# A first and a second attention: dense units dealt over the slots of the last and ahead of the first pair of heads

## What is computed

```python
# first block
h = rmsnorm(x, g_norm);  proj = h @ w_in            # u, v, gate, q, k, v, b_gate, gate_logits
y_a = chunked_spatial_gating(gelu(u), gelu(v), ...) * silu(a_gate)
y_b = dilated_attention(q, k, v) * silu(b_gate)     # 16 heads of 64, softmax, three dilations
g_a, g_b = split(sigmoid(gate_logits), 2)
x = x + (g_a * (y_a @ w_proj_a) + g_b * (y_b @ w_proj_b)) @ w_out
# second block: a state-space mixer, then a per-layer embedding with a sigmoid gate
# third block: stick-breaking attention over shared keys and values
k = rmsnorm(kv[..., :1024] per head);  q = rmsnorm(q per head) / 8
z = q @ k.T;  keep = sigmoid(-z);  weights = sigmoid(z) * (product of keep over the later keys)
y = (weights @ v) * silu(gate);  x = x + y @ w_out
```

## Time and profile before

| | |
|---|---|
| three timed runs | 3404.18, 3405.32, 3412.97 us; median 3405.32 |
| the profiled execution | 3399.16 us; span from first to last instruction 3397.7 us |
| busy | PE 92%, DVE 54%, ACT 41%, POOL 20% of the span |
| mean granted TensorE clock | 0.96 of full speed |
| first attention, pairs 0 to 6 | about 560 to 1080 us of the span, 74.0 to 74.6 us each |
| its last pair and what follows to the next stage | 1080.4 to 1152.2 |
| the stage after it | 1152.2 to 1325.9 |
| second attention: dense units of pair 0 | 2438.5 to 2488.1 |
| its pairs 0 to 6, then pair 7 | 2511.9 to 3100.5, then to about 3178 |

### The profile page before, as it was taken

How to read it: one execution, slowest core, us unless ns; L and a number is a source line. 1 busy time by engine, 2 the same in 40 slices (tenths; PEclk the granted TensorE clock), 3 DMA queues, 4 the chain that set the end, 5 groups by cost and what they waited for, 6 DMA issues and landing times. The chain is left out here.

```text
span 3397.7 us, 42014 instructions
## 1 busy us (share of the span) xinstructions
PE 3130.8 (92%) x15516; PEld 2609.2 (77%) x15516; DVE 1840.8 (54%) x2484; ACT 1404.4 (41%) x2100; POOL 667.5 (20%) x448
## 2 busy tenths in 40 slices
PE   6999999999999799879999999998889999997799
PEld 5788887888887587657777878777678888886677
DVE  4344223666666423356757566675447766776343
ACT  3333213555555422234334252434246666666331
POOL 3100002222222000211001020100224444443110
PEclk8999999999999899879999999999889999998899
DMA  2111222111111223002111121211211111111221
GB/s 96 41 48 41 74 68 72 59 57 57 57 59 67 75 70 109 32 27 71 53 58 56 50 75 44 75 44 62 82 32 38 38 38 38 38 38 44 113 73 56
DMA packets 54602, 197.36 MB, mean 58 GB/s; under 512 B 6304, under 2 KB 9248, under 8 KB 54176
## 3 DMA queue, kind: packets, MB, share of 16 engines
q1 hardware_dynamic: 45600, 164.66, 14.4%
q0 software_dynamic: 8832, 30.41, 2.9%
HBM read 165.56 MB, written 21.10 MB: 55 GB/s over the span
## 5 line engine op out<-in xcount | busy, mean ns | idle before, releaser
L114 ACT ACTIVATE whi<-wraw 128x1024 fp32r<-128x1024 f32 x208 | 218.4, 1050 | 451.3 <-PE a_D L127 59.2
L119 DVE TENSOR_TENSOR wlo<-wraw,whi 128x1024 fp32r<-128x1024 f32 x176 | 247.9, 1409 | 176.0 <-ACT whi L114 172.7
L125 PE MATMUL b_D<-x1hi,whi 128*128 128x512 f32 x640 | 255.9, 400 | 8.5 <-DVEq L999 6.6
L125 PE MATMUL ssm_D<-x1hi,whi 128*128 128x512 f32 x640 | 259.0, 405 | 4.6 <-DVEq L1748 4.6
L127 PE MATMUL ssm_D<-x1hi,wlo 128*128 128x512 f32 x640 | 252.0, 394 | 0.0
L126 PE MATMUL ssm_D<-x1lo,whi 128*128 128x512 f32 x640 | 251.9, 394 | 0.0
L126 PE MATMUL b_D<-x1lo,whi 128*128 128x512 f32 x640 | 251.3, 393 | 0.0
L127 PE MATMUL b_D<-x1hi,wlo 128*128 128x512 f32 x640 | 250.8, 392 | 0.0
L2178 DVE TENSOR_TENSOR_SCAN stick_keep<-stick_keep 128x896 f32<-128x896 f32 (+7 forms) x128 | 209.0, 1637 | 37.1 <-ACT stick_keep L2093 35.9
L125 PE MATMUL stick_D<-x1hi,whi 128*128 128x512 f32 x512 | 210.7, 412 | 7.0 <-DVE x1lo L152 7.0
L2321 POOL TENSOR_TENSOR stick_rows<-stick_rows,stick_keep 128x896 f32<-128x896 f32 (+7 forms) x128 | 157.9, 1236 | 295.2 <-DVE stick_keep L2178 290.1
(11 more groups left out here) (400 smaller groups left out, 8010.0 us busy)
## 6 DMA issues: line engine op xcount, KB each, us to landing
wraw<-w_dram SPq DMA_DIRECT2D x208, 512.0 KB, 3.5
sq<-acum_rows SPq DMA_DIRECT2D x32, 512.0 KB, 3.8
att_bias<-alibi_dram SPq DMA_DIRECT2D x16, 512.0 KB, 3.5
stack<-stack POOLq DMA_DIRECT2D x32, 256.0 KB, 3.6
x_sb<-xT_dram SPq DMA_DIRECT2D x8, 512.0 KB, 7.9
branch_a<-sq POOLq DMA_DIRECT2D x8, 512.0 KB, 3.5
y_b<-att_y POOLq DMA_DIRECT2D x8, 512.0 KB, 3.0
f<-y_b SPq DMA_DIRECT2D x2, 2048.0 KB, 9.4
```

The costliest lines, as they stand in the source:

```text
L114: act.activation(self.whi[:, s, :, :], self.wraw[:, s, :, :], ACT.Copy).then_inc(self.w_hi, 1)
L119: dve.tensor_tensor(self.wlo[:, s, :, :], self.wraw[:, s, :, :], self.whi[:, s, :, :].bitcast(F32), ALU.subtract).then_inc(self.w_lo, 1)
L125: pe.matmul(out, self.whi[:, s, w0, :], xhi[:, k, cols], start=start, stop=False)
```

## The change

Five edits.

1. *First attention, last pair.* `units` plays the full `UNITS` also in the last pair: the first four gate tiles of the next stage (g_b 0 to 3), whose weights, splits (ACT, POOL) and scaling (DVE) run as in any pair; 16 more units follow the last slot (the fifth gate tile, left in D). The scaled gate tiles lie where key, query, value and gate lay, and SP stores them to a DRAM tensor `gates`, behind its reload of y, which now stands behind three more weight loads.
2. *The stage after it.* It does gate and projection tiles 4 to 7 in turn as before ("early"), then projection tiles 0 to 3 alone ("late"), in alternate PSUM tensors, with the gate loaded by POOL from `gates`. The loops are written out. The first projection weight is split at the start of the stage. The order of the weights in DRAM follows.
3. *Second attention, ahead of pair 0.* Units, splits, scaling and the key, value and query steps are dealt over slots as in a pair, by new functions `ahead` on ACT and DVE. POOL hands on the key's parts ahead of two gains.
4. *Second attention, in the pairs.* ACT stores the second half of the key one slot later, behind the high parts of the weights; ACT squares the query in slot 17 for 16, and ACT and DVE split the weight of the pair after next in slot 17 for 16; DVE splits the next pair's second weight in slot 1, behind that slot's scan, for slot 0.
5. POOL's gain for the pair after next moves from slot 8 to slot 11.

```diff
# first attention: SP, POOL, TensorE
-                        if c % 2 == 1:
+                        if c % 2 == 1 and p < PAIRS - 1:
...
-                for p in range(PAIRS - 1):
+                for p in range(PAIRS):
                     pair(p)
                 sp.wait_ge(qk, 16 * (PAIRS - 1))
                 sp.wait_ge(y_left, 16 * (KT // 2))
                 sp.dma_start(y_first[:, 0:KT // 2, :], ...).then_inc(reloaded, 16)
+                for c, tile in enumerate((kT, qT, vT[:, :], gT[:, 0, :])):
+                    sp.wait_ge(evac, 8 * PAIRS + (2 * c + 4))
+                    sp.dma_start(gates[c, :, :], tile).then_inc(gates_left, 16)
                 sp.wait_ge(reloaded, 16)
+                sp.wait_ge(gates_left, 64)
...
-                    if p < PAIRS - 1:
-                        ahead(p + 1, (p + 1) % 2)
-                    else:
-                        split(p + 1, 1)
+                    ahead(p + 1, (p + 1) % 2, p < PAIRS - 1)
...
-                        n_units = UNITS[slot] if more else int(slot < 2 * KT)
-                        units(p + 1, u, u + n_units)
-                        u += n_units
+                        units(p + 1, u, u + UNITS[slot])
+                        u += UNITS[slot]
...
+                units(PAIRS + 1, 0, 2 * KT)
# the stage after it: POOL and TensorE
+                pool.dma_start(loaded_gate[0], gates[0, :, :]).then_inc(g_land[0], 16)
+                for i in range(KT):
+                    pool.wait_ge(m_done, i + 1)
+                    pool.dma_start(part_a, spill[(HALF + i) % KT, :, :]).then_inc(a_land, 16)
+                    if HALF <= i < KT - 1:
+                        pool.dma_start(loaded_gate[(i + 1) % 2], gates[i + 1 - HALF, :, :]).then_inc(...)
...
+                def late_tile(i):
+                    pe.wait_ge(K.w_lo, n0 + HALF + i + 1)
+                    if i == HALF:
+                        pe.wait_ge(g_scaled, HALF)
+                    else:
+                        pe.wait_ge(prod, i - 1)
+                    K.dense(pe, D2[:, :] if i % 2 else D[:, :], i % 2, yhi, ylo).then_inc(mm, 1)
+
+                for i in range(HALF):
+                    gate_tile(i)
+                    early_tile(i)
+                for i in range(HALF, KT):
+                    late_tile(i)
# second attention: TensorE ahead of pair 0
-                units(0, KT, 4 * 2 * KT)
+                u = KT
+                for slot in range(2, 19):
+                    units(0, u, u + UNITS[slot])
+                    u += UNITS[slot]
+                    aux(0, slot)
                 pe.wait_ge(masks, 4)
-                for slot in range(19):
-                    aux(0, slot)
# second attention: ACT
+                LATER = ("k_back1", "q_square")
...
+                def ahead(p, q, slot):
+                    if p == 0 and slot == AUX_SLOT["k_back1"] + 1:
+                        store_k(p, q, 1)
+                    if slot == half_done_slot(0, 1) + 1:
+                        split(p, 2)
+                    if slot == half_done_slot(1, 1) + 1:
+                        split(p, 3)
+                    if slot == AUX_SLOT["q_sum"]:
+                        square_of(p, q, 1)
+                        split(p + 1, 0)
+                    aux(p, q, slot)
...
                         for unit, g in turns_of(slot - 1):
                             high_weights(p, unit, g)
+                        if more and slot == AUX_SLOT["k_back1"] + 1:
+                            store_k(p + 1, 1 - q, 1)
                         if slot < 16:
                             weights(p, q, slot)
...
-                        if more and slot == 16:
-                            split(p + 2, 0)
# second attention: DVE
                     if slot == AUX_SLOT["q_sum"]:
+                        split(p + 1, 0)
                         inverse_q(p, q)
+
+                def ahead(p, q, slot):
+                    for c in range(4):
+                        for half in range(2):
+                            if half_done_slot(c, half) + 1 == slot:
+                                scale(p, q, c, half)
+                    if slot == 1 and p > 0:
+                        split(p, 1)
+                    if slot == half_done_slot(0, 1) + 1:
+                        split(p, 2)
+                    if slot == half_done_slot(1, 1) + 1:
+                        split(p, 3)
+                    aux(p, q, slot)
...
-                            if slot == 0:
-                                split(p + 1, 1)
...
-                        if more and slot == 16:
-                            split(p + 2, 0)
# second attention: POOL
-                        if more2 and slot in (8, 14):
+                        if more2 and slot in (11, 14):
                             gain(p + 2, int(slot == 14))
...
+                stack_parts(0, 0)
                 gain(1, 0)
-                gain(1, 1)
-                stack_parts(0, 0)
                 pool.wait_ge(zeroed, 1)
                 low_k(0, 0)
+                gain(1, 1)
```

More of the change, by code:

```diff
@@ L882, in pair @@
                                     high(p + 1, 1 - q, c)
-                        if more and slot == half_done_slot(2, 1) + 1:
+                        if slot == half_done_slot(2, 1) + 1:
                             split(p + 2, 0)
@@ L1026, in _ @@
             def _(sp):
-                for k in range(KT // 2):
-                    sp.dma_start(y[:, KT // 2 + k, :], y_dram[KT // 2 + k, :, :]).then_inc(y_land[k], 16)
-                K.load_ahead(sp, "pb")
+                for k in range(HALF):
+                    sp.dma_start(y[:, HALF + k, :], y_dram[HALF + k, :, :]).then_inc(y_land[k], 16)
+                with sp.Fori(1, 7) as i:
+                    for s in range(2):
+                        sp.wait_ge(K.w_lo, 2 * i + (n0 + s - 1))
+                        K.load_weight(sp, 2 * i + (n0 + s), s)
@@ L1051, in _, with early_tile @@
-                tile(0, first=True)
-                with pe.Fori(1, KT) as j:
-                    tile(j)
+                def early_tile(i):
+                    pe.wait_ge(K.w_lo, 2 * i + (n0 + 2))
+                    if i >= 1:
+                        pe.wait_ge(prod, i)
+                    K.dense(pe, D2[:, :], 1, yhi, ylo, y_lo if i == 0 else None).then_inc(mm, 1)
+                def late_tile(i):
[5 more added lines that the diff above has]
+                    K.dense(pe, D2[:, :] if i % 2 else D[:, :], i % 2, yhi, ylo).then_inc(mm, 1)
@@ L1086, in _ @@
                 dve.sem_inc(m_done, 1)
+                K.split_lo(dve, n0 // 2, 1)
                 for k in range(KT):
                     K.tile_lo(dve, ylo, yhi, y, k, None, y_hi, y_lo)
-                with dve.Fori(0, KT) as j:
-                    tile(j)
+                for i in range(HALF):
+                    early_tile(i)
+                for i in range(HALF, KT):
+                    late_tile(i)
 def stage_residual(K, name, src, xhi, xlo, f_sb, x_dram, src_dram=None):
@@ L2055, in aux @@
                     for step, when in AUX_SLOT.items():
-                        if when == slot and step in AUX:
+                        if when == slot and step in AUX and step not in LATER:
                             AUX[step](p, q)
@@ L2144, in _ @@
                         K.norm_root(act, pV, DM, sums_done, root_done)
-                for c in range(1, 4):
-                    split(0, c)
-                split(1, 0)
+                split(0, 1)
                 act.wait_ge(x_lo, KT)
@@ L2150, in _ @@
                 for slot in range(19):
-                    aux(0, 0, slot)
+                    ahead(0, 0, slot)
                 for p in range(PAIRS):
@@ L2257, in pair @@
                         if more:
-                            for c in range(4):
-                                for half in range(2):
-                                    if half_done_slot(c, half) + 1 == slot:
-                                        scale(p + 1, 1 - q, c, half)
-                            if slot == 0:
-                                split(p + 1, 1)
-                            if slot == half_done_slot(0, 1) + 1:
-                                split(p + 1, 2)
-                            if slot == half_done_slot(1, 1) + 1:
-                                split(p + 1, 3)
-                        if more and slot == 16:
-                            split(p + 2, 0)
-                        if more:
-                            aux(p + 1, 1 - q, slot)
+                            ahead(p + 1, 1 - q, slot)
                     if more:
@@ L2290, in _ @@
                 K.norm_copy(dve, scores, spread_done, r_done)
-                for c in range(4):
-                    for half in range(2):
-                        scale(0, 0, c, half)
-                    if c < 2:
-                        split(0, c + 2)
-                    if c == 2:
-                        split(1, 0)
                 for slot in range(19):
-                    aux(0, 0, slot)
```

(2 more changed lines are left out.)

118 lines of the change are left out of this document (62 added, 56 removed).

## The result

The changed kernel took 3323.60, 3328.39, 3329.12 and 3331.93 us, median 3328.76; the kernel before, on the same chip, 3404.18 to 3412.97, median 3405.07. The ratio is 0.9769, with a 95% interval of 0.9753 to 0.9785: faster by 76 us, where I had forecast 64.5.

A forecast was written before the change was run, and what follows sets the result against it. TensorE was taken to set the pace almost everywhere, so gains come only where it waits. Terms -31.4, -18.0 and -15.1 sum to -64.5, from 3405.3 to 3341 us; range 3329 to 3360.

The forecast's parts named there:

- First attention and projection: Last pair and next stage: later start +11.5, load +0.7, four tiles less -43.6; sum -31.4 us.
- pair 7's wait of 1.76 us: First attention's last pair: TensorE's wait behind ACT's two query copies was taken as gone, 1.76 us; bound: it stays.
- Ahead of pair 0: Second attention's start: dealt steps hide their waits under units, leaving 5.8 us of TensorE's own instructions; -18.0 us.
- (a): Second attention's pairs, slot 2: wait before the first weight transposition stays, POOL's product being held by DVE's split; 0.
- if POOL gets in first: Slot 2 of the second attention's pairs: POOL's product precedes DVE's split; -1.1 us a pair, -7.7 in all; chance 0.1.
- (b): Second attention's pairs, slot 10: moving POOL's gain frees the scan, so the wait before the transpositions goes; -4.4 us.
- (c): Second attention's pairs, slots 11 and 17: value products' waits for the weights' low part go; -10.7 us at most.
- The low clock: Slow clock at the second attention's first scores goes at no price; its pairs got no clock term.
- The shift to the median: Whole kernel: profiled execution lay 6.2 us below the timed median 3405.32, so the forecast started from 3405.3.
- The pairs giving nothing: Second attention's pairs: waits there yield no gain as other chains take over; 3356 us, chance 0.2.
- The stage's start: End of first attention: stores and reloads hold the next stage, or late tiles stall; 5 to 15 us, chance 0.08.
- slot-17 packing: Second attention's pair borders: query steps packed there delay the next first score; slower if over 7.1 us each, chance 0.02.

The follow-up runs named there:

- e1: First attention and projection stage as changed, second attention as in the kernel before; 3377.28 us, ratio 0.9898 to the kernel before.
- e4: The changed kernel again, unaltered, timed in a later group; 3328.16 us, ratio 0.9765 to the kernel before.
- e5: Changed kernel with gain, key's second store (behind slot 10's weight split), square and both weight splits back in their old slots in the second attention's pairs; 3359.84 us.
- e10: Changed kernel with only DVE's split of the next pair's second weight back in slot 0, ahead of the scan; 3333.12 us.
- e11: Changed kernel with DVE's split of the next pair's second weight in slot 2 for 1, behind the 128-column scan; 3320.47 us, ratio 0.9749 to the kernel before.
- e8: Changed kernel with only POOL's gain of a coming weight back in slot 8 for 11; 3332.21 us.
- e9: Changed kernel with only the key's second store back in slot 10, behind the weight split; 3334.68 us.
- e6: As e5 against the changed kernel, but the query's square and the weight split stay in slot 17; 3344.32 us.
- e7: Changed kernel with only the query's square and the weight split back in slot 16; 3340.36 us.
- e3: Changed kernel with the moves in the second attention's pairs undone, but the key's store ahead of slot 10's weight split, unlike the kernel before; 3366.67 us.
- e12: Changed kernel with DVE's split of the next pair's second weight in slot 3 for 1; 3341.51 us, ratio 0.9805 to the kernel before.
- e2: Second attention as changed, first attention, projection stage and weight order as in the kernel before; 3363.28 us, ratio 0.9859 to the kernel before.

## Why the prediction was right in sign and mechanism, and short in size

**First attention and projection, -31.4: right.** -32.6 in the trace, -32.1 in e1. The last value product came 1.7 us earlier than I had it. The pair that I took for the price, pair 6 at 74.40 us, has a low stretch (clock 0.98, shown above); pair 7 of the changed kernel ran without a wait and at 1.00 throughout. The way from the last value product to the y parts took 12.5 us for my 11.4, and ten tiles for fourteen gave 173.7 - 130.0 = 43.7 us, my 43.6 less 0.7 for the load. I had chosen to let pair 7's wait of 1.76 us go; it went.

**Ahead of pair 0, -18.0: right.** -17.0 in the trace, and 1.3 more to the first gate product, which I had put at no price: the clock of before was at 0.50 until 4 us behind the first score. From the stage's first dense product to the first score the profiled pair differs by 15.6; e4, without the low stretch that the changed kernel has there, by 17.3. By the medians against before (e1 -32.1, e5 -46.7) it is 14.6, with an interval of some 10 us around it.

**Pairs, (a) slot 2, 0: right to 1.9 us.** The wait stayed, at 1.44 for 1.76 us (e10: 1.9 us in all). The reason was the right one: the product is held by the split, 0.83 us of the 1.2 that I had. e11 tries the reason from the other side, and the gain that I had kept as a bound (-7.7, "if POOL gets in first") came in the form of -5.0 against the changed kernel, 6.9 against e10, once POOL did get in first. The bound had counted seven pairs, while this wait stands in six. The Trainium skill ("SBUF — State Buffer", section "Who interferes with whom") says that the two engines exclude each other on such operands and that the one issued first goes first; the trace agrees, with 2.83 and 1.19 us in the changed kernel, 2.00 and 2.27 us in e11.

**Pairs, (b) and (c), -4.4 and -10.7: right places, priced too low.** This is the first step that failed. The runs give 5.6 us (e8) for (b) and 8.4 (e9) + 6.6 (e6) = 15.0 for (c), 20.6 for my 15.1. I had added up the idle time that TensorE's waits show. But matmuls overlap: one of 512 columns is recorded with 0.39 us and follows the one before it by 0.23 (the rows at 2838.98 and 2839.21 above), and a wait also takes that overlap of some 0.16 us. The recorded waits of (b) and (c) are twenty, and 20 x 0.16 us are 3.2 of the 5.5 us missing. The rest stands in TensorE's busy time. The second of the seven pairs in the changed kernel, in e8 and in e9, the same 464 products:

```profile
2564.05:2644.27 80.22, 78.78 (x464) 68.53 (x464) 57.88 (x69) 53.32 (x83) 39.12 (x28) 1.00 0.13 39
```

```profile
2564.18:2645.32 81.14, 79.04 (x464) 68.63 (x464) 60.01 (x69) 53.39 (x83) 39.14 (x29) 1.00 0.14 39
```

```profile
2561.26:2642.68 81.42, 79.15 (x464) 68.52 (x464) 58.05 (x69) 53.49 (x83) 39.14 (x29) 1.00 0.13 40
```

One wait more raises the busy time by some 0.25 us in e8 and 0.37 in e9, and by 0.27 to 0.30 in the pairs of e7 that have no low stretch. With the recorded idle time (0.65 to 0.68, 0.81 and 0.72 us) that makes the 0.9, 1.2 and 1.0 us by which a pair is longer. Part of what goes beyond 0.16 is the first product behind a wait, which is recorded longer too in e7 and e9 (0.39 us for 0.28 at 256 columns, as in the row at 2840.54); e9 has two of them.

**The low clock, no term: the second step that failed.** The profiled execution of before had one low stretch in the seven pairs, that of e1, with the same pairs, five of seven, and e5 six; each costs 1.6 us, and the changed kernel has none. Shown is that such a stretch costs 1.6 us, that it comes behind the wait ahead of the head sums, though not in every pair and in e3 in none, and that the change removes it there (e5 against e6, e7 against e4). It does not remove those behind the waits of the first attention. In the profiled pair of kernels this step is worth 1.6 us. In the median it may be more: e1 and e5 had five and six stretches, but the timed runs leave a mean clock and no trace.

**The shift to the median: open.** I wrote that the profiled execution "lies 6.2 below the median of the three timed runs, 3405.32, so the forecast is 3405.3 - 64.5", which takes the 6.2 us for a constant. Four more low stretches in a median run would make 6.2 us, and then the change would remove them. But the blocks that are the same in all kernels were 5.8 us shorter in this execution than in the middle one of the 14 traces, and that difference the change leaves. e10 shows that this alone can do it: its profiled execution has no low stretch in pairs 0 to 6, and it lies 8.4 us below its median, with 1110.2 us in the same blocks. In the runs of before beside e1 to e12 the time goes with the clock: all those of at most 3401 us have a mean granted clock of 0.959 to 0.961, all those of at least 3412 us one of 0.954 to 0.957. It doesn't say in which block the clock was low. So the 6.2 us are not shown to be a step that failed.

**The sum.** The two traces account for the miss without that shift. The first attention and projection gave 1.2 us more than I had, the part ahead of pair 0 with the way to its first gate product 1.1 less, the seven pairs 9.2 more and the end 2.4 more: 11.7 of the 11.8 us between 64.5 and 76.3. The 9.2 are the 5.5 of (b) and (c), the 1.9 of (a), one low stretch of 1.6 and 0.2 left over. The 2.4 at the end are luck: e2 runs the same code there and had none of it. The trace of before held two hints of the clock that I passed over: one of its seven pairs took 85.2 us with clock 0.98, the others 82.7 to 84.0, and pair 6 of the first attention had 0.98 as well. I had read pairs 1 to 6 as one group. A pair of the second attention takes 80.2 us now for 83.6, where I had 82 for 84.

**The rivals.** The pairs giving nothing falls (24.3 us). The stage's start was 10.9 us late, not more, and the loaded gates stalled nothing. The slot-17 packing did not delay a score: in pairs 1 to 6 TensorE waits nowhere but in slot 2.

## What to carry to other kernels

A wait of TensorE costs its idle time, 0.25 to 0.4 us more for the overlap that it breaks (in e7, e8 and e9), and perhaps a stretch at half the clock. Here that came behind short waits with a group of tiny products after them, and behind waits of 1.8 to 2.2 us without such products; fill these waits first. Before a recurring stretch is read as one group, look at each repetition on its own, with its clock: two lengths of the same code are a cost that comes and goes. And before two profiled executions are compared as wholes, compare a part whose code is the same: here it differed by 9 us.

## What the runs showed of the hardware

- A wait of 0.72 us followed by sixteen products of two columns (1.85 us) was followed by a granted clock of 0.50 (1.2 GHz), for 3.4 us (twice 6.8), in one of seven pairs of before, five of e1, six of e5, four of e7 and none of e3. A wait of 0.81 to 0.99 us in front of the same group was followed by it in three of seven pairs of e12. Without a wait in front of it this group kept 1.00 in pairs 0 to 6 of the changed kernel, e2, e4, e6, e8, e9, e10 and e11.
- Waits followed by wider products: that of 0.81 us (e9) was followed by no such stretch in seven, nor was that of slot 2, 1.45 us in the changed kernel and 1.74 in e10. Those of 1.75 to 2.1 us in the first attention were followed by one in four of seven pairs of before and in one of e5; in e3 it came with the wait of 2.19 us in two of seven.
- What decides whether a given pair is hit I can't say: the identical instructions in the same order did both.
- A VectorE subtraction of 1024 columns with both inputs in SBUF and a GpSimd product of 1024 columns lengthen each other by the order of their start: 1.19 and 2.83 us with VectorE's first, 2.27 and 2.00 us with GpSimd's first (the changed kernel, e11).
- Blocks of the same code, from the output projection to the second attention, took 1110.1 to 1119.1 us in 14 traces.
